# Two layers of a mixer model: channel-major projections with both parts of x in one matmul, rotating through four PSUM banks

## What is computed

```
h = rms_norm(x, norm_w[l])
p = h @ w_in[l]                       # 2048 -> all the columns below
qa, ka, va, za, ub, zb, qkv_c, b_c, a_c, zc = _split_cols(p)
oa = sliding_window_sink_attention(rope(norm(qa)), rope(norm(ka)), va, sinks[l]) * silu(za)
ob = conformer_conv_module(ub, ...) * silu(zb)          # causal depthwise conv of 31 taps, layer norm
oc = gated_deltanet(qkv_c, b_c, a_c, ...) * silu(zc)    # conv of 4 taps, chunks of 64 tokens
x = x + concatenate([oa, ob, oc]) @ w_out[l]
```

## Time and profile before

| | us |
|---|---|
| median of 3 runs | 2363.49 (2362.72 to 2365.31) |
| profiled execution | 2363.78 |
| its span | 2362.0 |
| DVE busy | 1676.4 (71%) |
| ACT busy | 1289.5 (55%) |
| PEld busy | 2091.0 (89%) |
| DMA | mean 181 GB/s |

### The profile page before, as it was taken

One profiled execution on the slowest core, in us unless ns is written; L12 is line 12 of the kernel. 1 busy time (PEld: TensorE's weight loads), 2 busy tenths in 40 slices (PEclk: granted clock), 3 DMA queues, 4 the chain that ended last, 5 costly groups with the idle time before them and its releaser, 6 DMA issues.

```text
span 2362.0 us, 35804 instructions
## 1 busy us (share of the span) xinstructions
PE 2346.1 (99%) x15332; PEld 2091.0 (89%) x15332; DVE 1676.4 (71%) x1924; ACT 1289.5 (55%) x1442; POOL 0.2 (0%) x4
## 2 busy tenths in 40 slices
PE   9999999999999999999999999999999999999998
PEld 9999898899998988988888888888888888888886
DVE  6888768558986675667567576676668667678774
ACT  6554366545543655454444344365666575666673
POOL 0000000000000000000000000000000000000000
PEclk9999999999999999999999999999999999999999
DMA  7553344555533445555555555565455555555553
GB/s 259 200 190 127 126 143 145 194 214 183 190 130 109 143 161 207 189 185 189 196 188 187 196 189 187 195 219 196 160 181 195 194 182 195 191 185 195 204 206 125
DMA packets 64190, 428.03 MB, mean 181 GB/s; under 512 B 7200, under 2 KB 7840, under 8 KB 15136
## 3 DMA queue, kind: packets, MB, share of 16 engines
q1 hardware_dynamic: 61200, 414.48, 49.0%
q10 hardware_dynamic: 2832, 11.27, 1.3%
HBM read 421.53 MB, written 4.19 MB: 180 GB/s over the span
## 4 chain that ended last, share of the span: by engine, by line
PE 96%; DVE 1%; ACT 1%; DMA 1%; issue 0%; DVEq 0%; SPq 0%; ACTq 0%
PE PS L458 95%; PE PS L622 1%; ACT Q L1131 1%; DMA W<-in_wall 0%; DVE Q L1811 0%; PE PS L935 0%; PE PS L769 0%; PE PS L756 0%; DVE Q L1815 0%; PE PS L916 0%; DVE SM L1830 0%; ACT WH L1145 0%; DVE H L1811 0%; DMA TB<-in_tab 0%; DVE E L1811 0%
## 5 line engine op out<-in xcount | busy, mean ns | idle before, releaser
L1846 DVE TENSOR_TENSOR WL<-W,WH 128x2048 fp32r<-128x2048 f32 (+3 forms) x406 | 887.9, 2194 | 451.0 <-ACT WH L1145 450.4
L1145 ACT ACTIVATE WH<-W 128x2048 fp32r<-128x2048 f32 (+3 forms) x406 | 740.9, 1836 | 490.0 <-PE PS L458 429.0
L458 PE MATMUL PS<-H,WH 128*128 128x256 f32 (+1 forms) x4864 | 869.0, 325 | 0.5 <-ACT H L1131 0.5
L458 PEld LDWEIGHTS PS<-H,WH 128*128 128x128 f32 x4864 | 740.8, 191 | 72.3 <-issue 0.7
L458 PE MATMUL PS<-H,WL 128*128 128x256 f32 x3392 | 491.5, 285 | 0.9 <-DVE WL L1846 0.7
L458 PEld LDWEIGHTS PS<-H,WL 128*128 128x128 f32 x3392 | 446.9, 192 | 9.2 <-issue 2.3
L458 PE MATMUL PS<-WH,H 128*128 128x512 f32 (+1 forms) x1280 | 332.5, 379 | 0.0
L458 PEld LDWEIGHTS PS<-WH,H 128*128 128x128 f32 x1280 | 234.1, 188 | 46.0
L458 PE MATMUL PS<-WH,YS 128*128 128x512 f32 x1024 | 273.8, 389 | 0.0
L458 PEld LDWEIGHTS PS<-WH,YS 128*128 128x128 f32 x1024 | 192.2, 188 | 40.0
L458 PE MATMUL PS<-WL,H 128*128 128x512 f32 (+1 forms) x640 | 199.0, 388 | 0.0
(11 more groups left out here) (167 smaller groups left out, 1640.0 us busy)
## 6 DMA issues: line engine op xcount, KB each, us to landing
W<-in_wall SPq DMA_DIRECT2D x374, 1024.0 KB, 4.8
W<-in_wall SPq DMA_DIRECT2D x22, 512.0 KB, 3.5
W<-in_wall SPq DMA_DIRECT2D x8, 536.0 KB, 3.3
X<-in_x ACTq DMA_DIRECT2D x1, 2048.0 KB, 9.4
xsave<-X ACTq DMA_DIRECT2D x1, 2048.0 KB, 8.5
X<-xsave ACTq DMA_DIRECT2D x1, 2048.0 KB, 9.6
Q<-in_g_post ACTq DMA_DIRECT2D x8, 256.0 KB, 3.5
Q<-in_g_ple_out ACTq DMA_DIRECT2D x2, 1024.0 KB, 4.5
```

What stands on the lines that cost most here:

```text
L458: return e.matmul(o, l, r, start=start, stop=stop, skip_group_check=True)
L1145: e.activation(WH[:, s % NSPL, 0:m], W[:, c % NRAW, 0:m], ACT.Copy).then_inc(*up("hi", c))
L1846: e.tensor_tensor(WL[:, c % NRAW, 0:m], W[:, c % NRAW, 0:m], WH[:, s % NSPL, 0:m].bitcast(F32), ALU.subtract).then_inc(*up("lo", c))
```

## The change

In the first two layers all channel-major groups with split weights, but for the groups of the opening, go from mode `cm` to a new mode `rot`: ten groups in layer 0 (3 to 10, 13 and 15) and eleven in layer 1 (21 too).

- A unit of one tile by one k-tile is now one matmul of 512 columns (hi with HH and HL) and one of 256 (lo with HH), into a bank of its own. A group of 512 channels takes all four main banks, one of 256 takes two, a token-major group two. The starting bank moves on by that number, modulo four.
- In the first and the last chunk of a group the loop goes tile by tile: all matmuls of tile 0, then of tile 1, with a pump after each tile. Before a tile's first matmul PE waits for the last user of its bank (`taken`). In the last chunk tile 1 signals that the first pair is ready (`half`).
- In a bank the two halves of 256 columns are two partial sums. `rotated` on ACT copies the first half of a pair of banks (128 x 512) into SBUF; `rotated` on DVE then adds the second half and, in a further instruction, multiplies by the row factors. The bank is free after the add.
- The last tick of a group is taken apart on ACT and DVE: high or low, first pair, two pumps, second pair, two pumps. In groups of 256 channels it is: two pumps, the one pair, two pumps.

```diff
+            def taken(g, b, *keys):
+                i = (K.bank["main", g] + b) % 4
+                for k in users[i]:
+                    if K.has(*k):
+                        w.wait_ge(*to(*k))
+                users[i] = keys
...
+                def rot(self):
...
+                    def product(part, wt, kl, j, start, stop):
+                        x = self.src(k0 + kl)
+                        s = x[:, 0] if part == "lo" else x.rearrange("p k t -> p (k t)")
+                        return mm(self.bank[j][:, 512 - s.shape[1]:512], wt[:, kl, 128 * j:128 * j + 128], s,
+                                  start=start, stop=stop)
+
+                    if first or last:
...
+                        for j in range(tiles):
+                            if first:
+                                taken(self.g, j, ("ev_v", self.g, "sum", j // 2))
+                            for n_p, (part, wt) in enumerate(order):
+                                for kl in range(nk):
+                                    i = product(part, wt, kl, j, first and n_p == 0 and kl == 0,
+                                                last and n_p == 1 and kl == nk - 1)
+                                if tiles == 2:
+                                    pump()
+                            if last and tiles == 4 and j == 1:
+                                i.then_inc(*up("half", "pair", self.g))
+                            if tiles == 4:
+                                pump()
+                        i.then_inc(*up("chunk", c))
+                    else:
+                        for n_p, (part, wt) in enumerate(order):
+                            w.wait_ge(*to(part, c))
+                            for kl in range(nk):
+                                for r in self.ready(k0 + kl):
+                                    w.wait_ge(*to(*r))
+                                for j in range(tiles):
+                                    i = product(part, wt, kl, j, False, False)
...
+                                if (kl + 1) % (nk // 2) == 0:
+                                    pump()
```

On ACT:

```diff
+            def rotated(dst, nb=2):
+                for _ in range(3 if nb == 2 else 1):
+                    tick()
+                high(here["c"] + NSPL - 1)
+                here["c"] += 1
+                g = here["g"]
+                here["g"] += 1
+                w.wait_ge(*to("ev_v", g - 3 if g % 20 == 13 else g - 1))
+                for b in range(nb):
+                    if b == nb - 1:
+                        pump()
+                        pump()
+                    w.wait_ge(*(to("chunk", here["c"] - 1) if b == nb - 1 else to("half", "pair", g)))
+                    act(dst(b), duo(g, b)[0], ACT.Copy, "ev_a", g, b, lag=0)
+                pump()
+                pump()
+                return g
```

On DVE:

```diff
+            def rotated(dst, nb=2):
+                for _ in range(3 if nb == 2 else 1):
+                    tick()
+                low(here["c"] + NSPL - 1)
...
+                for b in range(nb):
+                    if b == nb - 1:
+                        pump()
+                        pump()
+                    w.wait_ge(*to("ev_a", g, b))
+                    tt(dst(b), dst(b), duo(g, b)[1], ALU.add, "ev_v", g, "sum", b)
+                    tt(dst(b), dst(b), rb(2), ALU.mult, *(("ev_v", g) if b == nb - 1 else ()))
+                pump()
+                pump()
+                return g
...
-                    g = group(4 if i < 4 else 2)
-                    scaled(lambda b: RAW[:, 4 * i + 2 * b:4 * i + 2 * b + 2, 3:259], g, 2 if i < 4 else 1)
+                    g = rotated(lambda b: RAW[:, 4 * i + 2 * b:4 * i + 2 * b + 2, 3:259], 2 if i < 4 else 1)
```

More of the change, by code:

```diff
@@ L317, in bank @@
         def bank(g, b):
+            if g < POOL_G[0]:
+                at = 512 * ((K.bank["main", g] + b) % 4)
+                return PS[:, at:at + 512]
             if g in POOL_G or g in LRU_G:
@@ L468, in side @@
                 return PS[:, 2048 + 512 * i:2560 + 512 * i]
+            def taken(g, b, *keys):
[4 more added lines that the diff above has]
+                users[i] = keys
             def released(g):
+                if g < POOL_G[0]:
+                    for b in range(2):
+                        taken(g, b, ("ev_a", g), ("ev_v", g))
+                    return
                 before = (g - 3, g - 2) if g in (POOL_G[1], LRU_G[1]) else (g - 2,)
@@ L488, in __init__ @@
                     self.src, self.ready, self.ncols, self.mode, self.nk = src, ready, ncols, mode, nk
+                    if self.g < POOL_G[0]:
+                        K.bank["main", self.g] = here["b"]
+                        here["b"] = (here["b"] + (ncols // 128 if mode == "rot" else 2)) % 4
+                    if mode == "rot":
+                        self.bank = [bank(self.g, b) for b in range(ncols // 128)]
+                        return
                     self.bank = [bank(self.g, b) for b in range(ncols // 128 if mode == "wide" else 2)]
@@ L544, in feed @@
                         here["c"] += 1
+                def rot(self):
+                    c = here["c"]
+                    name, l, k0, nk, c0, n = chunks[c]
+                    tiles = self.ncols // 128
+                    hi, lo = (v[:, i, 0:nk * n].rearrange("p (k n) -> p k n", k=nk)
+                              for v, i in ((WH, split_no[c] % NSPL), (WL, c % NRAW)))
+                    order = (("hi", hi), ("lo", lo)) if here["up"] else (("lo", lo), ("hi", hi))
+                    here["up"] = not here["up"]
+                    first, last = self.done == 0, self.done + nk == self.nk
+                    def product(part, wt, kl, j, start, stop):
[4 more added lines that the diff above has]
+                    if first or last:
+                        for part, _ in order:
+                            w.wait_ge(*to(part, c))
[18 more added lines that the diff above has]
+                        for n_p, (part, wt) in enumerate(order):
+                            w.wait_ge(*to(part, c))
+                            for kl in range(nk):
+                                for r in self.ready(k0 + kl):
+                                    w.wait_ge(*to(*r))
+                                for j in range(tiles):
+                                    i = product(part, wt, kl, j, False, False)
+                                if n_p == 1 and kl == nk - 1:
+                                    i.then_inc(*up("chunk", c))
+                                if (kl + 1) % (nk // 2) == 0:
+                                    pump()
+                    self.done += nk
+                    here["c"] += 1
@@ L1489, in block1 @@
                 skip(1)
-                group(2)
+                rotated(lambda b: Y[:, 4:6, :], 1)
                 def ysplit(k, lag, *ready):
```

58 lines of the change are left out of this document (36 added, 22 removed).

## The result

The changed kernel takes 2409.7 us (2407.4 to 2413.9, 5 runs) against 2364.0 of the kernel before on the same chip: a ratio of 1.020, interval 1.018 to 1.021. It is slower, as forecast with a chance of 0.80, but by 45.7 us and not 32.4. Applied to the median that stood ahead of the prediction, the ratio gives 2410.05, just outside the range that ended at 2410. The profiled execution took 2409.7 us with a span of 2407.9.

A forecast was written before the change was run, and what follows sets the result against it. PE, busy 2346.1 of 2362.0 us, was taken as the bound, so matmul time saved and waits added count one for one. 2363.8 - 15.0 + 41.4 (waits) + 6.0 (clock) = 2396.2, forecast 2396; 8-in-10 range 2371 to 2410.

The forecast's parts named there:

- matmul time saved: First two layers: 1152 units of one tile by one k-tile, each 13 ns shorter, 15.0 us.
- (a): Group 3's tile 2 waits for group 2's banks, read late behind a late chunk's split: 4.1 us a layer.
- (b): End of group 3: second pair's copy and add stand behind the decay-factor step; stall 2.4 us a layer.
- (c): End of group 8: DVE's full queue after its normalisers delays the first add; group 9 stalls 8.6 us a layer.
- (d): End of group 9: eviction behind side steps needing matmuls issued after group 10's tiles 0 and 1; 3.0 us a layer.
- (e): Group 13's tiles 2 and 3 wait 0.8 us for group 12's banks, group 14 1.8 for group 13's, each layer.
- (f): Granted clock drops to 1.2 GHz after the long waits (a) and (c): four drops of 1.5 us, 6 us, bounds 0 and 18.
- rival 3: DVE becomes the bound in groups 4 to 8 too, 1.2 us for each of five groups: 2408; chance 0.07.
- Partly: First rival: (a) and (c) hold but let DVE catch up, so (b), (d), (e), (f) vanish: 2374; chance 0.18.
- Faster: Second rival: evictions come in time, with some 7 us of DVE's steps behind group 8's first add: 2349; chance 0.14.
- Rival 4: The clock falls after the eight shorter stalls too, 8 x 1.5 us more: 2408; chance 0.04.
- rivals 3 to 5: Three slower cases, each 2408; the fifth: pitches as with isolated matmuls, saving 3 us instead of 15, chance 0.01.

The follow-up runs named there:

- experiment 1: Changed kernel with PE kept busy by unread products ahead of four of its waits in each layer: 2401.7 us.
- e11_c_cured: Changed kernel with two mask multiplies, group 8's last lo split and seven convolution instructions taken out of DVE's queue ahead of group 9's first add: 2397.6 us.
- experiment 2: Changed kernel with DVE work ahead of group 9 moved away in three cumulative runs: mask multiplies 2403.6 us, also lo split 2400.6, also convolution steps 2397.6.
- experiment 5: Changed kernel with DVE's and ACT's order changed at the ends of groups 2, 3, 9: 2396.0 us; with the new form in seven groups a layer only: 2368.9.
- experiment 4: Changed kernel with group 15 (and 35) alone put back to the old form: 2409.8 us.
- experiment 6: Changed kernel with the new form only in groups 5, 6, 7, 9 of each layer: 2361.2 us; without 9: 2360.1; then with 21: 2359.4.
- experiment 3: Changed kernel with group 8 (and 28) alone put back to the old form: 2396.1 us.

## Why the prediction was right in kind and too low in size

Slower was right, and so were the places and the order of the named waits. The sum was 13.5 us too low, enough to put the time just outside the range. The steps that failed are four: side work behind the evictions was put at nothing and cost 4.8 us; the named waits were put at 41.4 and cost 44.9; the clock was put at 6.0 and cost 8.9; and the matmul time saved was put at 15.0 and is 12.7. Both layers together, in us; the measured terms are what groups grew by beyond their saving, with the clock's share taken out by experiment 1:

| term | predicted | measured |
|---|---|---|
| matmul time saved | -15.0 | -12.7 |
| (a) group 3, tile 2 | 8.2 | 8.4 |
| (b) group 4, tile 2 | 4.8 | 5.9 |
| (c) group 9 | 17.2 | 17.5 |
| (d) group 10, tile 2 | 6.0 | 7.7 |
| (e) groups 13 and 14 | 5.2 | 5.4 |
| transposes of group 10, attention, group 21 | none | 4.8 |
| (f) half clock | 6.0 | 8.9 |
| sum | 32.4 | 45.9 |

The medians differ by 45.7.

**What bounds the kernel** held: PE's wait went into the time one for one, and no wait appeared at the ends of groups 4 to 7 where half a microsecond was to spare (rival 3 is out). That the spare time was no more than that shows in e11_c_cured, where more of DVE's work lies in groups 5 and 6 and PE waits there.

**Saved matmul time.** The pitch was read rightly; 13 ns was rounded up from 12.7, which is 0.4 us. The failed step is the nothing put on a group's first and last chunk. In groups of 512 channels they take 5.61 and 5.59 us where an inner one takes 5.57 and the wide ones of the second half 5.56. It isn't the many matmuls in a row into one bank: in groups of 256 channels 16 of them go there in a row, and the last chunk takes 5.56 us, the first 5.59. It goes with the short runs: matmuls of 512 columns start 232 to 233 ns apart in runs of four and 228 in the long ones. Over 30 such chunks that is 1.1 us, and the inner ones add 0.3; group 21, with 0.2 us of wait in its first chunk, saves 0.52 us and not 0.71. A different order of the same matmuls should have had a bound, not a zero. The rule of the Trainium skill ("TensorE: Matmul & The Clock Gate", Back-to-back issue gap), which it gives for an isolated matmul, would have had 3 us saved (2.5 ns a unit; the prediction's 2.6 is a slip). The trace gave four times that, so the rule's spacing doesn't describe this stream.

**The waits that were named.** The mechanism of three is shown: (c) by experiment 2, (b) and (d) by experiment 5; (a) is shown in half, by experiment 5, and (e) was not tried. They measure 44.9 against 41.4. The gaps between matmuls themselves add up to 42.8; the other 2.1 us is what the groups grow by beyond their gaps. It isn't a fixed price of a wait: it is 0.4 us a layer in group 10 and 0.3 at (e), but nothing at (c), and in experiment 5, with (d) gone, group 10 is still 0.3 us longer than its saving and its transposes explain. No run looks for its cause. Of the gaps (d) and (b) were the furthest off, 3.45 against 3.0 and 2.82 against 2.4.

**The waits that were not.** The sentence that failed is "By itself it is hidden behind PE; its price is in the waits below". I asked who waits for the banks, and not who waits for the side steps that DVE and ACT do after an eviction. A copy, an add and a multiply at the end of group 15 stand ahead of the softmax (1.6 us a layer, experiment 4), those of group 9 ahead of what the transposes of group 10 need (0.7, experiment 6). PE didn't wait at either place in the kernel before, but little was to spare, and that could have been read from its trace: 0.06 us at the attention's first transposes (the rows in experiment 4), some 0.5 us at those of group 10. The rest of the 4.8 us is mostly the smaller saving of group 21.

**The clock.** That it falls after long waits, and what that costs, was right in kind; experiment 1 shows it by equal stretches of waiting with a busy PE. The mis-sized step is "four such drops: 6 us". There were five, and a drop isn't always as long as the one in the rows: at (c) it lasted 10.2 and 6.8 us and cost 2.9 and 1.5. There the clock fell 4.1 and 3.7 us before the wait was over, and what it cost is about half of the 6.1 and 3.1 us that were left. The rule of the Trainium skill that was weighed against the change ("TensorE: Matmul & The Clock Gate", psum-queue depth-cycling) names the trouble rightly, short idleness between groups as banks are cycled and lost clock behind it; its size here is 8.9 us of 45.7.

**The rivals.** "Partly" fell in its strong form: (c) didn't make (b), (d) and (e) vanish; but it did take 0.7 to 1.0 us off (d) (experiment 3). "Faster" named a condition, some 7 us of DVE's work out of the way, that wasn't met; e11_c_cured, where it was met by 8.6 us, took 2397.6 and not 2349, because (a), (b), (d) and (e) don't hang on it. Rival 4 was half true: once in the changed kernel, and more often in the variants, half clock followed a wait as short as (b) or (d).

**The range** ended at 2410 because rivals 3 to 5 all did. They were taken one at a time, on top of a sum in which every term was a best guess; but every term of the sum erred on the same side. The forecast alone was given as 2384 to 2408; added up as they are said there, a fifth more on (a) to (e) and 12 for (f) make 2410.5, and with the 18 that (f) had as its bound 2416.5.

## What to carry to other kernels

Before a change makes a later engine's result wanted sooner, list for that engine everything it has in its queue at that moment, and then, for each added instruction, who waits for what stands behind it, consumers of side work included: here the second list was missing, at 2.4 us a layer. Moving work behind an eviction pays only if the engine has slack in the next group; otherwise the same lateness shows up one group on. And where a form saves 0.7 us a group and a single missed eviction costs 2 to 9, use it only where the margin is seen in the timeline: three groups in ten gave 3 us of the 12.7 that the form can save, and nearly all that any mixture here got.

## What the runs showed of the hardware

Half clock goes with a wait of PE of a given length in one place and not in another. In the thirteen profiled kernels, counting PE's waits of 1.2 us and more between 50 and 2300 us: none of 40 waits under 2 us had it during the wait or right behind it, 3 of 4 at 2.05 us, 1 of 11 at 2.8, 2 of 3 at 3.1 to 3.2, 5 of 9 at 3.45, and all 36 from 3.7 us up. In about half of these 47 the clock fell before the wait was over. The stretches last 3.4, 6.8 or 10.2 us, and the same wait got different ones: (a), at 4.1 us, 3.4 in most kernels and 6.8 in two. So two kernels with the same waits can differ by a few microseconds by this alone, which is the size of several effects in this study.

A weight chunk doesn't always land after the same time. In all thirteen profiles the chunk behind group 21's wait was issued 11.9 us before the end of group 20. In eleven it landed 9.1 us later and ACT waited 6.2 us for it; in two it took 10.4 and 10.6, and ACT waited 7.5 and 7.6. With its banks wanted at once (nine kernels), group 21 made PE wait 1.4 and 1.5 us in these two and 0.2 us in the other seven. Why the chunk came later there isn't known.
